# Stores of gated hidden blocks on their own semaphore, norm roots ahead of low parts, and operand loads ahead of residual loads

## The reference

```
def swiglu(h, w_gate, w_up, w_down):
    return (jax.nn.silu(h @ w_gate) * (h @ w_up)) @ w_down
...
        x = x + 0.5 * swiglu(rmsnorm(x, norm_ffn1[l]), w_ffn1_gate[l], w_ffn1_up[l], w_ffn1_down[l])
        x = x + hybrid_mixer(rmsnorm(x, norm_mix[l]), w_in[l], attn_sink[l], ...)
        x = x + 0.5 * swiglu(rmsnorm(x, norm_ffn2[l]), w_ffn2_gate[l], w_ffn2_up[l], w_ffn2_down[l])
    return rmsnorm(x, norm_final)
```

## Time and profile before

| what | value |
|---|---|
| median of 3 runs | 2461.09 us (2459.72 to 2462.23) |
| the profiled execution's own time | 2464.09 us |
| its span in the profile | 2462.3 us |
| PE busy | 2320.7 us (94%) |
| DVE busy | 1190.6 us (48%) |
| ACT busy | 727.8 us (30%) |
| POOL busy | 254.1 us (10%) |

### The profile page before, as it was taken

How to read it: one execution, slowest core, us unless ns; L and a number is a source line. 1 busy time by engine, 2 the same in 40 slices (tenths; PEclk the granted TensorE clock), 3 DMA queues, 4 the chain that set the end, 5 groups by cost and what they waited for, 6 DMA issues and landing times. The chain is left out here.

```text
span 2462.3 us, 32516 instructions
## 1 busy us (share of the span) xinstructions
PE 2320.7 (94%) x12960; PEld 2011.8 (82%) x12960; DVE 1190.6 (48%) x2022; ACT 727.8 (30%) x1366; POOL 254.1 (10%) x188
## 2 busy tenths in 40 slices
PE   3998999999989999999999889999999999999998
PEld 3998999999968877777778778888888888877887
DVE  5555555555546585856555674511111111136576
ACT  5322222222233344644443211311111111123343
POOL 5000000000000001111001222211111121100000
PEclk7999999999999999999999999999999999999999
DMA  3133222222286565422425824122222222246555
GB/s 121 35 99 100 72 72 73 86 76 72 87 304 219 178 195 151 145 96 83 134 80 171 277 108 159 35 80 81 79 74 72 104 78 89 74 147 198 188 177 174
DMA packets 227191, 298.08 MB, mean 121 GB/s; under 512 B 22880, under 2 KB 141664, under 8 KB 227040
## 3 DMA queue, kind: packets, MB, share of 16 engines
q1 hardware_dynamic: 216672, 275.01, 34.8%
q10 hardware_dynamic: 10368, 20.98, 2.3%
HBM read 205.49 MB, written 87.16 MB: 119 GB/s over the span
## 5 line engine op out<-in xcount | busy, mean ns | idle before, releaser
L1963 PE MATMUL ps<-h_hi,w_hi 128*128 128x512 f32 (+1 forms) x1488 | 536.4, 361 | 5.3 <-ACT q_rot L1139 2.5
L1964 PE MATMUL ps<-h_lo,w_hi 128*128 128x512 f32 (+1 forms) x1488 | 528.7, 355 | 0.0
L1965 PE MATMUL ps<-h_hi,w_lo 128*128 128x512 f32 (+1 forms) x1488 | 528.5, 355 | 0.0
L2030 PE MATMUL ps<-hs,w_hi 128*128 128x384 f32 (+1 forms) x1232 | 391.3, 318 | 50.5 <-DVE u L1530 42.9
L2031 PE MATMUL ps<-hs,w_hi 128*128 128x384 f32 (+1 forms) x1232 | 389.0, 316 | 0.0
L1963 PEld LDWEIGHTS ps<-h_hi,w_hi 128*128 128x128 f32 x1488 | 282.6, 190 | 65.0 <-issue 18.7
L2040 PE MATMUL ps<-w_hi,dh 128*128 128x512 f32 x770 | 304.0, 395 | 18.3 <-DVE w_lo L1596 11.8
L1965 PEld LDWEIGHTS ps<-h_hi,w_lo 128*128 128x128 f32 x1488 | 282.6, 190 | 39.9
L1964 PEld LDWEIGHTS ps<-h_lo,w_hi 128*128 128x128 f32 x1488 | 283.0, 190 | 37.6
L2032 PE MATMUL ps<-hs,w_lo 128*128 128x384 f32 (+1 forms) x992 | 313.0, 316 | 0.0
L2042 PE MATMUL ps<-w_hi,dh 128*128 128x512 f32 x770 | 302.6, 393 | 0.0
(11 more groups left out here) (210 smaller groups left out, 2858.9 us busy)
## 6 DMA issues: line engine op xcount, KB each, us to landing
dr<-hid_mid SPq DMA_DIRECT2D x154, 320.0 KB, 3.1
w_raw<-in_w_ffn_down SPq DMA_DIRECT2D x176, 256.0 KB, 3.4
hid_mid<-st SPq DMA_DIRECT2D x88, 320.0 KB, 3.5
w_raw<-in_w_ffn_gate SPq DMA_DIRECT2D x44, 512.0 KB, 4.0
w_raw<-in_w_ffn_up SPq DMA_DIRECT2D x44, 512.0 KB, 4.8
hid_mid<-sg SPq DMA_DIRECT2D x66, 320.0 KB, 2.6
w_raw<-in_w_in SPq DMA_DIRECT2D x14, 512.0 KB, 4.7
proj<-stage ACTq DMA_DIRECT2D x24, 256.0 KB, 3.2
```

The lines of the kernel that those rows point to most:

```text
L1963: mm(out, hi, rhs_hi, start=first, stop=False)
L1964: mm(out, hi, rhs_lo, start=False, stop=False)
L1965: return mm(out, lo, rhs_hi, start=False, stop=last)
L2030: mm(out, hi[:, k, :], b_hi, start=k == 0 and j in (GP1, GP6, GP5), stop=False, skip_group_check=True)
```

## The change

It has four parts.

1. **Stores.** The three stored blocks of `sg1` are issued one by one, each when its product is complete, and in the first gate-up phase that is during the odd pair (`store_block`, `store_hidden(i)`). The four sums go out one by one as DVE forms them (`store_sums`), and count on a semaphore of their own, `sums_stored`. The silu of the next group waits for the three block stores and for the sums to be formed, no longer for the stores of the sums. The same is done in the second gate-up phase.
2. **Roots.** POOL does the roots of pairs 0, 1 and 2 before the first low parts.
3. **Down phases.** The load of hidden block 4 and its weight stand ahead of the last group's stores. The ten residual loads of the first down phase go out at every second step, 1 to 19, each in the order in which it is used, and the gain load at step 20. `keep_p1` stands ahead of the split of step 14 on ACT. DVE forms the last group's sums ahead of the preparation of step 3 (first phase) or 2 (second phase). `share_p1` moves from slots 12 to 16 to slots 17 to 21.
4. **Semaphores.** Some are merged (`A2["prod"]` into `S["mult"]`, `G["masking"]` into `G["masked"]`), with the same events waited for.

```diff
-            def store_hidden(f, i):
-                sp.wait_ge(hid_summed, 4 * (GROUPS * f + i + 1))
-                for p, block in ((DP1, hid(f, 0)), (DP2, hid(f, 1)), (DP4, hid(f, 3)), (DP5, ST[f][:, 0, :]),
-                                 (DP6, ST[f][:, 1, :]), (DP7, ST[f][:, 2, :]), (DP3, ST[f][:, 3, :])):
-                    sp.dma_start(hid_mid[p, i], block).then_inc(hid_stored, 16)
+            def store_block(f, i, p, q):
+                sp.dma_start(hid_mid[p, i], hid(f, q)).then_inc(hid_stored, 16)
+
+            def store_hidden(i):
+                up = NP * (2 * i + 1)
+                for p, q, j in ((DP1, 0, GP2), (DP4, 3, GP5), (DP2, 1, GP4)):
+                    sp.wait_ge(S["mult"], G_MULT[(up + j, 1)])
+                    store_block(0, i, p, q)
+
+            def store_sums(f, i):
+                for j, p in enumerate((DP5, DP6, DP7, DP3)):
+                    sp.wait_ge(hid_summed, 4 * (GROUPS * f + i) + j + 1)
+                    sp.dma_start(hid_mid[p, i], ST[f][:, j, :]).then_inc(sums_stored, 16)
...
                 if q % 2 and q >= 3:
-                    store_hidden(0, q // 2 - 1)
+                    store_sums(0, q // 2 - 1)
                 load_gu1(2 * q + 1)
                 if q + 1 < G_PAIRS:
                     load_gu1(2 * q + 2)
+                if q % 2 == 0:
+                    store_hidden(q // 2 - 1)
...
-            store_hidden(0, GROUPS - 1)
-            sp.wait_ge(S["done"], len(GORDER))
-            load_gain(gain1[:, :], norm_mix[0:1, :])
...
-                if 1 <= n <= TT:
-                    sp.dma_start(x_tile(1, n - 1), x_rows(n - 1).rearrange("p (k n) -> p k n", n=P)
-                                 ).then_inc(x_loaded[n - 1], 16)
+                if n == 0:
+                    store_hidden(GROUPS - 1)
+                    store_sums(0, GROUPS - 1)
+                if n % 2 and n // 2 < TT:
+                    t = N1_ORDER[n // 2]
+                    sp.wait_ge(S["done"], len(GORDER))
+                    sp.dma_start(x_tile(1, t), x_rows(t).rearrange("p (k n) -> p k n", n=P)).then_inc(x_loaded[t], 16)
...
-            first_roots(0)
-            first_roots(1)
+            for t in range(3):
+                first_roots(t)
             for t in range(HT):
                 first_t_lo(t)
-                if t + 2 < HT:
-                    first_roots(t + 2)
+                if t + 3 < HT:
+                    first_roots(t + 3)
...
                     if q and c == 0 and j == GP2:
-                        act.wait_ge(hid_stored, 16 * NP * (q // 2))
+                        act.wait_ge(hid_stored, 48 * (q // 2))
+                        act.wait_ge(hid_summed, 4 * (q // 2))
...
             for m in range(GROUPS * DP4 + GROUPS - D_TAIL):
+                if m == GROUPS:
+                    keep_p1(0)
                 if m + D_LEAD < D_STEPS and m:
                     d_hi(0, m + D_LEAD)
-                if m == GROUPS:
-                    keep_p1(0)
...
-                if p == DP2 and 1 <= i <= HT:
+                if p == DP2 and i >= GROUPS - HT:
                     for which in range(3):
-                        share_p1(f, i - 1, which)
+                        share_p1(f, i - GROUPS + HT, which)
```

More of the change, by code:

```diff
@@ L390, in build @@
         NF = named("norm_final", "sum root scaled")
-        A2 = named("ffn2", "gate up silu prod")
+        A2 = named("ffn2", "gate up")
         S = named("gateup", "done kept added silu mult")
@@ L827, in _ @@
                 if v % 4 == 1 and v >= 9:
-                    store_hidden(1, v // 4 - 2)
+                    i = v // 4 - 2
+                    sp.wait_ge(S["mult"], len(G_MULT) + 6 * (i + 1))
+                    for p, q in ((DP1, 0), (DP4, 3), (DP2, 1)):
+                        store_block(1, i, p, q)
+                    store_sums(1, i)
                 load_gu2(v)
@@ L832, in _ @@
                     load_gain(gain2[:, :], norm_final.rearrange("(a d) -> a d", a=1))
-            store_hidden(1, GROUPS - 2)
+            sp.wait_ge(S["mult"], len(G_MULT) + 6 * (GROUPS - 1))
+            for p, q in ((DP1, 0), (DP4, 3), (DP2, 1)):
+                store_block(1, GROUPS - 2, p, q)
+            store_sums(1, GROUPS - 2)
             for n in range(2):
@@ L852, in _ @@
                     load_down(1, n + D_LEAD + 1)
+                if n == 0:
+                    sp.wait_ge(S["mult"], len(G_MULT) + 6 * GROUPS)
+                    for p, q in ((DP1, 0), (DP4, 3), (DP2, 1)):
+                        store_block(1, GROUPS - 1, p, q)
+                    store_sums(1, GROUPS - 1)
                 if n > GROUPS * DP7 and n % 2 and n // 2 - GROUPS * DP7 // 2 - 1 < HT:
@@ L1369, in silu @@
                 if i and t == 0 and c == 0:
-                    act.wait_ge(hid_stored, 16 * NP * (GROUPS + i))
+                    act.wait_ge(hid_stored, 48 * (GROUPS + i))
+                    act.wait_ge(hid_summed, 4 * (GROUPS + i))
                 act.wait_ge(A2["gate"], s + 1)
-                nc.scalar.activation(sg2[:, t, c0:c0 + n], ps[:, GU + 2 * (s % 2), 0:n], ACT.Silu).then_inc(A2["silu"], 1)
+                nc.scalar.activation(sg2[:, t, c0:c0 + n], ps[:, GU + 2 * (s % 2), 0:n], ACT.Silu).then_inc(S["silu"], 1)
             for t in range(TT):
@@ L1395, in _ @@
             for m in range(GROUPS * DP4 + GROUPS - D_TAIL):
+                if m == GROUPS:
+                    keep_p1(1)
                 if m + D_LEAD < D_STEPS:
                     d_hi(1, m + D_LEAD)
-                if m == GROUPS:
-                    keep_p1(1)
                 t, phase = divmod(m - GROUPS * DP7, 2)
@@ L1649, in _ @@
                 g_evict(s, c)
-                if c:
-                    if s + G_LEAD < G_STEPS:
-                        g_prepare(s + G_LEAD)
-                    elif s + D_LEAD + 1 >= G_STEPS:
-                        d_prepare(0, s + D_LEAD + 1 - G_STEPS)
-                g_mult(s, c)
+                if c and s + G_LEAD < G_STEPS:
+                    g_prepare(s + G_LEAD)
+                g_mult(s, c)
+                if c and s + 1 == G_STEPS:
+                    for which in range(4):
+                        hid_sums(0, GROUPS - 1, which)
+                if c and s + D_LEAD + 1 >= G_STEPS:
+                    d_prepare(0, s + D_LEAD + 1 - G_STEPS)
                 if q % 2 == 0 and q and j < 2:
@@ L1663, in _ @@
                     v.tensor_scalar(neg_sinks[:, :], sinks[:, :], -1.0, None, ALU.mult).then_inc(const_set, 1)
-            for which in range(4):
-                hid_sums(0, GROUPS - 1, which)
             for m in range(GROUPS * DP4 + GROUPS - D_TAIL):
@@ L1940, in _ @@
                         product(i, t, c)
-                        if i == GROUPS - 1 and t == 1:
+                        if i == GROUPS - 1 and t == 1 and c < 2:
                             d_prepare(1, c)
@@ L1944, in _ @@
                     hid_sums(1, i, which)
+            d_prepare(1, 2)
             for m in range(GROUPS * DP4 + GROUPS - D_TAIL):
@@ L2248, in scores @@
                 if c:
-                    pe.wait_ge(G["masked"], NCH * h + c)
+                    pe.wait_ge(G["masked"], 3 * (NCH * h + c))
                 elif h:
```

33 lines of the change are left out of this document (18 added, 15 removed).

## The result

The changed kernel takes 2371.04 us (median of four runs, 2368.07 to 2372.90), the kernel before 2461.37 (median of four runs): a ratio of 0.9633, 95% interval 0.9616 to 0.9649, so 90 us less. The prediction was 2370, range 2358 to 2392. The profiled execution took 2370.79 us with a span of 2369.0; before they were 2464.09 and 2462.3.

The account below looks back on a forecast made before the run. The prediction took the kernel to be bound by TensorE (PE busy 2320.7 of 2462.3 us). 62.1 + 5.1 + 14.1 + 12.2 - 2.4 = 91.1 us off 2464.09 gave 2373.0 profiled, median 2370, range 2358 to 2392.

Parts of the forecast that it names:

- The gate-up stalls, 62.1 us: First gate-up phase: ten PE stalls go with the clock they cost, 42.3 us idle plus 19.8 us clock.
- the DVE named in rows 2 is the last link of a chain that begins at the stores: Gate-up, pair 4: late sum stores delay silu, weight cast, DVE's low part and addition; PE stood 3.73 us.
- The weight load, slack 1.7 us: Gate-up: up unit lands 3.72 us after issue, DVE's addition is ready at 186.1, PE runs out at 187.83.
- the weight load becomes the stall: Rival, 20%: gate-up's up unit lands later than 3.72 us after issue; 2400 us, half of that loss 2385.
- The start, 5.1 us: Start: earlier roots on POOL save 1.5 us in the first period and 1.8 in each of the next two.
- some two of the four low parts collide: Start, second and third periods: POOL's low parts collide with DVE, costing 2.5 us of a possible 4.1 to 4.3.
- The first and second down phase, 14.1 and 12.2 less the shares: Both down-phase starts: all idle and clock loss goes, 14.1 and 12.2 us, less 2.4 for the moved shares.
- The shares, 2 x 1.2 us: Down phases, step 22: moved shares delay the residual additions, so PE stalls 1.2 us in each phase.
- Part 4, 0: The merged semaphores change no event: 0 us.

Follow-up runs that it names:

- sums together: Changed kernel, but the first gate-up phase's four sum stores are issued together after the fourth sum; block stores stay early: 2388.45 us.
- three, load first: Changed kernel with seven gate-up stores batched after the fourth sum, up weight unit issued ahead of them, silu waiting for three block stores: 2390.70 us.
- three, late: Changed kernel with seven gate-up stores batched after the fourth sum, ahead of the weight load; silu waits for three block stores and that sum: 2430.58 us.
- all, late: Changed kernel with part 1 undone in the first gate-up phase: seven stores batched ahead of the weight load, silu waiting for all seven: 2431.01 us.
- all, load first: Changed kernel with seven gate-up stores batched after the fourth sum, up weight unit issued ahead of them, silu waiting for all seven: 2444.32 us.

## Why the prediction was right, and where its steps were not

- **The gate-up stalls, 62.1 us:** 63.3 by the events, 60 by the run that undoes part 1. Idle time and clock are priced rightly from the windows. But the reading that gave the chain was half of it, and so the term came out in part by luck. The prediction said "the DVE named in rows 2 is the last link of a chain that begins at the stores" and followed it through the silu alone. In pair 4 a second chain, through the weight load, ended within 0.2 us of it: DVE's weight sum started at 189.54, 5.29 us after the issue at 184.25, and the same load landed 5.14 us after its issue in the run where DVE stood waiting for it. The forecast came out because the change shortens both chains.
- **The weight load, slack 1.7 us:** mis-sized, 0.6 measured. I took the landing of 3.72 us from the pair before, where the queue ahead was empty. In the even pairs it is 4.07 to 5.55 us in the new trace, 5.13 in pair 4; the issue itself came 0.4 us after the sum ended instead of 0.75. The rival "the weight load becomes the stall" was nearer than its 1.7 us said: a load issued 1.7 us later brought the stall of 1.06 us.
- **The start, 5.1 us:** 7.4 in the profiled execution. The step was "some two of the four low parts collide". The first period gave 2.5 (31.05 to 28.52, the start of the second pair's block operations), not 1.5, and the next two 2.2 each (43.37 to 38.68, then 55.10 to 48.25), not 1.8. In these two the scalings took 4.25 us, 1.8 more than the 2.47 without the collision, where 2.5 had been taken off for it, and POOL's four low parts 5.94 and 5.96, 1.0 more than alone. What is left of the 7.4, 0.5 us, came behind the three periods.
- **The first and second down phase, 14.1 and 12.2 less the shares:** 13.0 and 11.5 us against 12.9 and 11.0. The size was right, the cause wrongly assigned: part 3 with its order is worth 12 us in both phases together, and 10 more come with the early stores of the last group (22.0 by the traces with both undone). The other 2.5 of the 24.5 us are not explained by a run; they are in the second down phase.
- **The shares, 2 x 1.2 us:** a stall is there, 0.63 and 0.62 us, and each down phase is 1.0 us shorter without it. The additions began at 676.49, 1.84 us behind the start of step 22 at 674.65 (when ACT was released), where I had counted 2.2.
- **Part 4, 0:** nothing speaks against it; it wasn't tried alone. Nor was the spread of the residual loads.
- **The mixer and the second gate-up phase**, on which the prediction said nothing, gave back 1.9 us of the profiled execution; 1.5 of it is one wait for a stage buffer (L1177) of 2.7 us where it was 1.2, and in eight of the twelve experiments it is 1.2 to 1.4 again. It goes with none of the edits: this stretch takes 1213.5 to 1217.7 us in the eleven traces in which its code is that of the changed kernel, so the 1.9 can't be told from that spread.

The second chain could be seen in the trace of before in two other pairs, 6 and 12, where DVE waits for the up unit itself, and PE's stalls behind these waits, 5.13 and 5.15 us, are the two longest of the ten:

```profile
245.58 0.69 DVE L1496 TENSOR_TENSOR w_sum<-w_raw 128x512 f32<-128x512 f32 x1 [0.22 <-DMA w_raw<-in_w_ffn_up]
...
411.97 0.69 DVE L1496 TENSOR_TENSOR w_sum<-w_raw 128x512 f32<-128x512 f32 x1 [0.84 <-DMA w_raw<-in_w_ffn_up]
```

Sum of the measured terms: 63.3 + 7.4 + 13.0 + 11.5 - 1.9 = 93.3 us, against 91.1. The errors of the terms were 2.3 at most. That the median came within 1 us is partly luck: the profiled execution was 2.2 us faster than the 2373.0 forecast for it, and the 3.0 us by which the one of before lay over its median did not come again (2370.79 against a median of 2371.04).

## What to carry to other kernels

When a stall's chain is followed back, look at every input of the last waiting operation, and at when each would have been there alone: two chains that start at one event can be of one length, and then taking away one of them brings nothing. A store that is issued when its data is complete frees the queue for the load behind it, and lands sooner for whoever waits on it. With the stores early it made no difference here which of them the silu waited for (2371 us either way); with them late and the load ahead it made 54 us (2391 and 2444). And a landing time is to be read in the place that it is used for, behind the same transfers.

## What the runs showed of the hardware

The clock makes long stalls dearer than short ones. For the runs with stalls in the gate-up phase the table has PE's ten waits for the additions, their sum and range, the mean granted clock from 75 to 590 us, and by how much the stretch from the first full step to the first down matmul is longer than the 521.5 us without stalls:

```
run                      ten stalls   single stalls   clock   stretch longer by
sums together            13.2         1.1 to 2.1      1.00    15.6
three, load first        17.3         1.2 to 3.5      0.99    24.0
three, late              41.2         3.6 to 5.1      0.97    60.5
all, late                42.2         3.8 to 5.1      0.96    61.3
all, load first          51.0         4.7 to 6.0      0.95    75.2
```

In the first two runs the seventeen stalls of 1.1 to 1.7 us cost their own length: the next stall began 49.4 us after the end of each. The other three, of 1.8, 2.1 and 3.5 us, cost 1.5, 2.3 and 5.0 us more than their length. In the last three runs, where every stall is of 3.6 us or more, each cost 1.9 to 2.4 us on top of its length on average, as PE then fell from 2.4 to 1.2 GHz for a while (in pair 4 of the trace of before a matmul of 384 columns took 0.52 us behind the stall, 0.33 us at the full clock). The windows (stretch, length, PE's busy time, PEclk, DMA share, GB/s) of the two kinds of run, first the kernel with all stores late, then the one with the sums together:

```profile
75.00:590.00 515.00, 477.17 (x3140) 0.96 0.25 79
```

```profile
75.00:590.00 515.00, 500.95 (x3405) 1.00 0.28 87
```

The second thing is the price of a DMA that is put ahead of others on one queue: in pair 4 one weight unit of 512 KB ahead of seven stores moved the landing of the third store by 1.6 us and that of the seventh by 1.2, as the silu that waits for them shows.
